# Two transformer blocks on one core: the buffers that TensorE streams are placed at eight different distances, counted modulo 512 bytes, from the buffers of the weights

## The reference

```
h = rms_norm(x, norm_mix_pre);  proj = h @ w_in
mix = concat(retention(...), nsa(...)) @ w_out            # first block
x = x + rms_norm(mix);  x = x + rms_norm(conv_ffn(rms_norm(x), w_up, conv, w_down))
x = x + ab_mixer(rms_norm_2(x, ab_norm), ...)             # second block, layer 0
x = x + square(relu(rms_norm_2(x, g) @ ffn_w1)) @ ffn_w2
x = x + mla_mixer(rms_norm_2(x, c_norm), ...)             # layer 1
x = x + square(relu(rms_norm_2(x, g) @ ffn_w1)) @ ffn_w2
out = rms_norm_2(x, final_norm)
```

## Time and profile before

| | us |
|---|---|
| median of 2 runs | 1883.99 |
| lowest and highest | 1883.8, 1884.19 |
| span of the profiled execution | 1881.6 |
| TensorE (matmul) busy in it | 1841.5 |
| VectorE busy | 1155.1 |
| ScalarE busy | 743.9 |

### The profile page before, as it was taken

How to read it: one execution, slowest core, us unless ns; L and a number is a source line. 1 busy time by engine, 2 the same in 40 slices (tenths; PEclk the granted TensorE clock), 3 DMA queues, 4 the chain that set the end, 5 groups by cost and what they waited for, 6 DMA issues and landing times.

```text
span 1881.6 us, 24672 instructions
## 1 busy us (share of the span) xinstructions
PE 1841.5 (98%) x8818; PEld 1481.6 (79%) x8818; DVE 1155.1 (61%) x1651; ACT 743.9 (40%) x1099; POOL 226.6 (12%) x228
## 2 busy tenths in 40 slices
PE   8999999999999999999999999999999999999998
PEld 6787558888888887887888888887666788888887
DVE  7867876784765778777543434476777553444344
ACT  6365334442432454655432232334544342323232
POOL 0021453000000030000000000003477200000000
PEclk9999999999999999999999999999999999999999
DMA  6332022233333233311333333332110123333332
GB/s 215 92 133 68 1 79 90 84 94 102 92 99 101 90 113 90 90 57 56 96 101 98 93 101 94 95 100 79 46 34 25 55 90 101 95 95 100 92 98 90
DMA packets 48217, 165.68 MB, mean 88 GB/s; under 512 B 5376, under 2 KB 7424, under 8 KB 48000
## 3 DMA queue, kind: packets, MB, share of 16 engines
q1 hardware_dynamic: 46512, 161.27, 28.3%
q10 hardware_dynamic: 1616, 3.22, 0.5%
HBM read 162.38 MB, written 2.10 MB: 87 GB/s over the span
## 4 chain that ended last, share of the span: by engine, by line
PE 85%; DVE 9%; ACT 3%; issue 2%; POOL 1%; DMA 0%; DVEq 0%; ACTq 0%; SPq 0%; POOLq 0%
PE ps L695 25%; PE ps L697 25%; PE ps L696 25%; PE ps L1089 2%; DVE w_lo L2225 1%; PE ps L989 1%; DVE qk_c L2995 1%; POOL x L608 1%; ACT w_hi L1564 1%; DVE tmp L2262 1%; PE ps L917 1%; PE ps L970 1%; PE ps L1059 1%; PE ps L1355 0%; PE ps L886 0%
## 5 line engine op out<-in xcount | busy, mean ns | idle before, releaser
L1564 ACT ACTIVATE w_hi<-raw 128x1024 fp32r<-128x1024 f32 x279 | 296.1, 1061 | 760.7 <-PE ps L697 760.4
L695 PE MATMUL ps<-h_hi,w_hi 128*128 128x512 f32 (+1 forms) x1288 | 507.9, 394 | 8.1 <-DVE w_lo L2506 7.6
L697 PE MATMUL ps<-h_hi,w_lo 128*128 128x512 f32 (+1 forms) x1288 | 499.0, 387 | 0.0
L696 PE MATMUL ps<-h_lo,w_hi 128*128 128x512 f32 (+1 forms) x1288 | 498.9, 387 | 0.0
L2225 DVE TENSOR_TENSOR w_lo<-raw,w_hi 128x1024 fp32r<-128x1024 f32 x279 | 345.5, 1238 | 119.7 <-ACT w_hi L1564 118.3
L695 PEld LDWEIGHTS ps<-h_hi,w_hi 128*128 128x128 f32 x1288 | 242.5, 188 | 62.1 <-DVE w_lo L2506 7.6
L697 PEld LDWEIGHTS ps<-h_hi,w_lo 128*128 128x128 f32 x1288 | 242.3, 188 | 50.0
L696 PEld LDWEIGHTS ps<-h_lo,w_hi 128*128 128x128 f32 x1288 | 242.6, 188 | 49.2 <-issue 1.9
L695 PE MATMUL ps<-hid_hi,w_hi 128*128 128x512 f32 (+1 forms) x716 | 273.6, 382 | 1.7 <-DVE w_lo L2225 0.9
L697 PE MATMUL ps<-hid_hi,w_lo 128*128 128x512 f32 (+1 forms) x716 | 272.6, 381 | 0.0
L696 PE MATMUL ps<-hid_lo,w_hi 128*128 128x512 f32 (+1 forms) x716 | 272.6, 381 | 0.0
(11 more groups left out here) (435 smaller groups left out, 2547.6 us busy)
## 6 DMA issues: line engine op xcount, KB each, us to landing
raw<-in_panels SPq DMA_DIRECT2D x295, 512.0 KB, 3.6
x_in<-in_x SPq DMA_DIRECT2D x8, 256.0 KB, 5.5
x<-in_x ACTq DMA_DIRECT2D x1, 2048.0 KB, 9.7
out<-y SPq DMA_DIRECT2D x16, 128.0 KB, 1.8
first<-in_first SPq DMA_DIRECT2D x1, 1568.0 KB, 11.4
raw<-in_panels SPq DMA_DIRECT2D x2, 256.0 KB, 4.6
second<-in_second ACTq DMA_DIRECT2D x1, 512.0 KB, 3.5
small<-in_small ACTq DMA_DIRECT2D x1, 328.0 KB, 4.2
```

The lines of the kernel that those rows point to most:

```text
L695: nc.tensor.matmul(out, a[0], b[0], start=start, stop=False)
L696: nc.tensor.matmul(out, a[0], b[1], start=False, stop=False)
L697: return nc.tensor.matmul(out, a[1], b[0], start=False, stop=stop)
L1564: nc.scalar.activation(w_high(panel, i), raw[:, panel % 4, :], ACT.Copy).then_inc(w_hi_ready, 1)
```

## The change

No computation, operand size, engine or wait is changed. Unused tensors (`before_high`, `before_low`, and so on) are allocated ahead of the high and low parts of `h`, `hid`, `aq` and `cq`; `hid_hi` becomes a view that begins four elements (16 bytes) into a wider tensor; and the block of small constants loses 56 unused columns (224 bytes per partition), which moves everything behind it down.

```diff
--- before.py
+++ after.py
@@ -72,7 +72,7 @@
     ("ident", 128), ("ones", 128), ("g_mix_post", 8), ("g_ffn_pre", 8), ("g_ffn_post", 8),
     ("gn", 4), ("cmp_pos", 64), ("conv0", 132), ("g_ab", 8), ("conv1", 40), ("gate_b", 1), ("g_head", 4),
     ("g_c", 8), ("g_cq", 3), ("g_ckv", 2), ("g_ffn1", 8), ("g_ffn2", 8), ("g_final", 8), ("freq", 1),
-    ("rope_sign", 1), ("minus_half", 16), ("head_row", 4), ("shift_rows", 3), ("g_v", 4), ("spare", 57), ("g_mix_pre", 8))
+    ("rope_sign", 1), ("minus_half", 16), ("head_row", 4), ("shift_rows", 3), ("g_v", 4), ("spare", 1), ("g_mix_pre", 8))
 FIRST, FIRST_N = columns(("rope_c", 512), ("rope_s", 512), ("cmp_c", 32), ("cmp_s", 32), ("decay", 2048))
 SECOND, SECOND_N = columns(("sgu_b", 512), ("ws_t", 512))
 MASKS, MASKS_N = columns(("ident", 128), ("k_q", 128), ("q_k", 128), ("cmp_q_k", 128), ("cmp_k_q", 512))
@@ -189,8 +189,10 @@
     raw = sb("raw", [P, 4, PANEL], F32)
     w_hi = sb("w_hi", [P, 2, PANEL], F32R)
     w_lo = sb("w_lo", [P, 2, PANEL], F32R)
+    before_high = sb("before_high", [P, 32], F32)
     ev = sb("ev", [P, 4, S], F32)
     h_hi = sb("h_hi", [P, KD, S], F32R)
+    before_low = sb("before_low", [P, 48], F32)
     h_lo = sb("h_lo", [P, KD, S], F32R)
     tmp = sb("tmp", [P, 4, S], F32)
     sq = sb("sq", [P, 2, S], F32)
@@ -244,7 +246,10 @@
             gate_rows = term.rearrange("p n s c -> p (n s c)")[:, 0:S]
     x = sb("x", [P, KD, S], F32)
     with ExitStack() as c:
-        hid_hi, hid_lo = sb("hid_hi", [P, 8, S], F32R, c), sb("hid_lo", [P, 8, S], F32R, c)
+        before_hid_high = sb("before_hid_high", [P, 112], F32, c)
+        hid_hi = sb("hid_hi_wide", [P, 8 * S + 8], F32R, c)[:, 4:8 * S + 4].rearrange("p (k s) -> p k s", k=8)
+        before_hid_low = sb("before_hid_low", [P, 56], F32, c)
+        hid_lo = sb("hid_lo", [P, 8, S], F32R, c)
         hid_f = sb("hid_f", [P, 2, S], F32, c)
         conv_t = sb("conv_t", [P, 2, S], F32, c)
         act_t = sb("act_t", [P, S], F32, c)
@@ -252,7 +257,10 @@
         ff_spread = sb("ff_spread", [P, 2, S], F32R, c)
     with ExitStack() as c:
         second = sb("second", [P, SECOND_N], F32, c)
-        aq_hi, aq_lo = sb("aq_hi", [P, 8, S], F32R, c), sb("aq_lo", [P, 8, S], F32R, c)
+        before_aq_high = sb("before_aq_high", [P, 80], F32, c)
+        aq_hi = sb("aq_hi", [P, 8, S], F32R, c)
+        before_aq_low = sb("before_aq_low", [P, 56], F32, c)
+        aq_lo = sb("aq_lo", [P, 8, S], F32R, c)
         av = sb("av", [P, NT, 4, 129], F32, c)
         ao = sb("ao", [P, 4, S], F32, c)
         a_t = sb("a_t", [P, 2, NT, 64], F32, c)
@@ -274,7 +282,10 @@
             den = sb("den", [P, 8], F32, cc)
     with ExitStack() as c:
         c_raw = sb("c_raw", [P, 5, S], F32, c)
-        cq_hi, cq_lo = sb("cq_hi", [P, 5, S], F32R, c), sb("cq_lo", [P, 5, S], F32R, c)
+        before_cq_high = sb("before_cq_high", [P, 32], F32, c)
+        cq_hi = sb("cq_hi", [P, 5, S], F32R, c)
+        before_cq_low = sb("before_cq_low", [P, 120], F32, c)
+        cq_lo = sb("cq_lo", [P, 5, S], F32R, c)
         q_hi, q_lo = sb("q_hi", [P, 4, S], F32R, c), sb("q_lo", [P, 4, S], F32R, c)
         k_hi, k_lo = sb("k_hi", [P, 4, S], F32R, c), sb("k_lo", [P, 4, S], F32R, c)
         quad_hi, quad_lo = sb("quad_hi", [P, S], F32R, c), sb("quad_lo", [P, S], F32R, c)
```

## The result

The changed kernel takes 1908.45 us (two runs, 1907.72 to 1909.19) against 1883.99: 24.5 us more, a ratio of 1.013 with a 95% interval of 1.0101 to 1.0159. The interval leaves out 1, so the kernel is slower, though by less than 2%, and the time lies above the predicted range, which ended at 1896. The span of the profiled execution is 1905.8 us, 24.2 us longer than before, so the time was lost inside the span.

What follows compares the result with a forecast made beforehand. The prediction took a full-clock stream of TensorE matmuls to bound the kernel, busy 1841.5 of 1881.6 us. Its terms summed to 0 against that span, giving 1884.5 us with the 2.4 us around it; range 1877 to 1896.

Steps and rivals of the forecast that it cites:

- the value for the distances in the first edit: Moved h, hid, aq, cq: cost per matmul taken as 0, from 352 against 256, between bounds of -76 and +32 us.
- the addition: Every TensorE matmul: 13.3 ns, or 32 ticks, above one column per tick; seemed to shrink with fewer weights, 9.3 ns in the compressor.
- The bound on the slower side: Matmuls with changed distance: pace just after a break, 232 ns, +5.6 ns each x 5724 = +32 us.
- The count of 5724: TensorE matmuls of 512 columns whose own distance changes: 5724 of 6384, leaving out 660 where hid_lo keeps 256.
- The count of 6384: 512-column TensorE matmuls using a shifted tensor, five groups of trios (h, hid, w past h, aq, cq): 1447 us, 77% of span.
- Rival 2: TensorE stream doesn't settle after breaks: +32 us, 1916, or +76, 1960; chance 0.10 within 2%, mild form included, 0.06 beyond.
- mild form: Unsettled stream only in hid_hi, moving in 1320 matmuls: +7 us, 1891; its chance is included in the 0.10 within 2%.
- Rival 3: Change doesn't do what it says in one stretch: hid_lo keeps 256, w and h change sides; no price or chance of its own.
- Rival 1: Weight and moving readers no longer meet, the addition goes: -76 us, 1808; chance 0.05 beyond 2%, 0.05 a part within.
- register instructions: Two on VectorE, in two loops: costed at nothing; 14 us if TensorE waited every time in the first feed-forward.
- other addresses: Everything else moves 224 bytes down or 96 to 704 up; VectorE and ScalarE have slack: 0.
- smaller DMA: Constants' DMA shrinks from 656 to 600 columns: -0.36 us at most on that DMA, 0 for the kernel.

Runs made afterwards that it cites:

- e9: Not the kernel: bare TensorE stream, 60 blocks of 48 equal matmuls at varied distances, columns, weights and types, no other engine working; float32r 512 columns at distance 0: 226.7 ns.
- e2: Against the kernel before: h at 128/128, hid at 192/192, aq and cq at 384, high and low parts alike; 1916.59 us, ratio 1.0173.
- e8: Against the kernel before: h at 96, hid at 8 bytes from the weights, high and low parts alike; 1920.50 us, ratio 1.0193.
- e4: Against the kernel before: only hid changed, to 16/256 as the change has it; h stays at 0/0; 1892.33 us, ratio 1.0047.
- e6: Against the kernel before: h at 64, hid at 32 bytes from the weights, high and low parts alike; 1904.90 us, ratio 1.0111.
- e10: Not the kernel: bare TensorE stream in the product's order, 4-byte distance steps, unlike high and low distances, shifted low weights; none of 113 blocks below 226.67 ns.
- e1: Against the kernel before: all tensors behind the constants 224 bytes lower, distances between them unchanged; 1884.89 us, ratio 1.0005.
- e3: Against the kernel before: h and hid at 0/256, aq and cq at 0, with the smaller block of constants; 1883.34 us, ratio 0.9998.

## Why the prediction was wrong, point by point

- *What bounds the kernel, and that only the pace of the stream can change*: right. The 24.8 us of the five groups are all of the loss.
- *The step that failed* is the value for the distances in the first edit: "I take 0, the value of 352 against 256, as the row nearest in kind", with the reading before it, "that the distance changes the order of long and short steps, and not their sum". The rows were read rightly: the earlier trace rows are both 120.0 ns, and e9 gives 120.0 at 0 and at 96. But they were of 256 columns, and the sum was over matmuls of 512. e9 shows that the two don't rank the distances alike: at 512 columns 96 costs 6.7 ns more than 0, at 256 nothing, and 160 costs 7.6 ns more at 512 and 2.7 ns less at 256. The compressor's panels, with 126 and 62 weights, were no witness either: 64 weights and 512 columns step at 228.3 to 231.1 ns in e9, with 230.0 at 0. That also contradicts the reading that the addition shrinks with the number of weights: at a distance of 0, 128 weights have 226.7 ns.
- The bound on the slower side, +5.6 ns from the earlier trace rows, held for this change: the groups went up by 3.4 to 5.1 ns but for cq, where it was 2.1. That was in part luck, since the row shows a stream after a break and not another distance: e2 (33 us slower) and e8 (37 us) lie beyond its 32 us, and single bare blocks reach +15.5 ns. It was the choice between the bounds that went wrong.
- *The count of 5724* left out the 660 matmuls of `hid_lo`, since their own distance stays. e4 shows them 4 ns longer. The price is the trio's: 24.5 us over 6384 are 3.8 ns each. The count of 6384 also left out 96 matmuls of 512 columns that use shifted tensors, w past cq (they are in the earlier trace rows) and aq past aq; together they take less than 0.1 us more.
- *Rival 2*, the stream that doesn't fall back into the even pace, is what happened, at 24.5 of its 32 us. Its mild form, hid alone, was put at +7 us; e4 measured 8.6. Its picture was half right: there is no lack of a lock. At most distances off the multiples of 256 the stream locks as well, into other patterns, all of them slower, and sometimes into one of two.
- *Rival 3* said that it makes no difference when w and h change sides. At 128 it makes none, but in e6 it turns 64 into 192, and 229 ns into 233.3.
- *Rival 1* had no case: none of the bare float32r blocks of 512 columns, 113 in e10 and 40 in e9, goes below the 226.7 ns of 0. The 13.3 ns themselves stay unavoided.
- The *register instructions*, the *other addresses* and the *smaller DMA* at nothing: right. Idle time behind `hid_lo` is 0.7 us, e1 shows the addresses (`hid_f` and what lies behind it move by 800 bytes, not by at most 704, at no price either), and e1 and e3 hold the smaller DMA. The first matmul did start 0.4 us earlier, but in e4, which keeps the larger DMA, it starts 0.2 us earlier too, so that this isn't clear of noise.

What stays open: why the distance between weights and moving data matters in float32r and not in bf16, and why the ranking differs between 256 and 512 columns. The runs show that the loss goes with where these two operands stand to each other, with TensorE alone at work. That their two reads hinder each other fits this and isn't shown.

No run points to a kernel faster than the one before. Matmuls of 256 columns would gain up to 2.7 ns at 160, about 0.7 us for the 264 of them here; that is less than the 1.9 us by which e3's interval is uncertain, and they share their tensors with the 512-column ones, which would lose. It wasn't tried with tensors of their own.

## What to carry to other kernels

When float32r matmuls of 512 columns and 128 weights follow each other without a break, put what moves at a multiple of 256 bytes from what is loaded as weights, for high and low parts alike; a pad or a view that begins a few elements in cost 1.6 to 15.5 ns of 227 on every matmul of the trio in the blocks measured here. Read such a price from starts in the timeline over stretches of a hundred steps, from the very shape on which the sum rests: a row of half the columns gave the wrong answer here. A step times a count then overstates the whole where the stream breaks off often (26.1 against 24.8 us). And where one stretch shows two paces, look for repeating patterns, and at how the stretch began, before looking for traffic of another engine.

## What the runs showed that I had not expected

- float32r, 512 columns, 128 weights: 226.7 ns at a distance of 0 modulo 256 bytes, 228.3 to 242.2 ns at all others tried; in bf16 215.8 ns at each of four distances.
- 4 bytes matter: 237.4 ns at 4, 233.3 at 8, 228.9 at 12.
- Matmuls lock into repeating patterns, often of a few steps (one to five in 32 of e9's 36 blocks of float32r with 512 columns and 128 weights, within 1 ns), and one distance can have two (228.9 and 232.2 ns at 128/320, 228.9 and 233.3 at 64). They were held for up to 383 steps; where a stretch begins can pick one.
- At 256 columns 0 isn't best: 120.0 ns against 117.3 at 160; nor is it with 64 weights and 512 columns: 230.0 ns against 228.3 at 64.
